# A two-layer trunk with a mixture of experts: the experts' gate and up products as plain fp32 in TensorE's four column groups, and x stored by ScalarE

## The chip, the cores and the metric

The kernel runs on one core of one Trainium2 chip, as one launch. The metric is the time of the launch on the device in microseconds (us); the median of three runs is what a change is judged by. A profile is one execution of its own, with one row for each instruction and each DMA packet. TensorE has two rows in it: PE for the products and PEld for the loads of their stationary side.

## The reference, cut to what matters

Two layers work on 640 tokens of 1,024 features: 512 latent ones and 128 context ones. Each layer has attention and a second mixer, and then a mixture of 16 experts. This part is what the change touches:

```
aff = softmax(x @ w_router, over tokens)
gate, idx = top_k(aff, cap)                # 64 latent + 16 context rows for an expert
xs  = x[idx]                               # 80 x 1024
hid = silu(xs @ w_gate) * (xs @ w_up)      # 1024 x 512 each
y   = (hid @ w_down) * gate                # 512 x 1024
out = zeros.at[idx].add(y)
```

Everything is fp32. An expert has 6 MB of weights and each is used once for a layer, so both layers together load 192 MB of them.

## The kernel before

**An expert's work.** The weights come in six blocks of 128 x 2048 values (1 MB): `g0 g1` (gate), `u0 u1` (up), `d0 d1` (down). To multiply fp32 values in one pass for each pair of operands, the kernel splits every value into a rounded part (`hi`, type fp32r) and a rest (`lo`), and computes `hi*hi + hi*lo + lo*hi` (`passes`, L1051). ScalarE writes `w_hi` from the loaded block (`expert_split`, L1953), VectorE subtracts it and writes `w_lo` (L2076). Three places of each of `w_hi` and `w_lo` go round (`SPLITS`). The 80 gathered rows are turned by TensorE (`turn_rows`, L1527) and split in the same way (`rows_split`), as is the turned hidden row (`hidden_split`). In `rows_times` (L1543) the 80 turned rows are the stationary side and 512 columns of a block the moving side: 8 slices of the 1,024 features, 3 passes, so 24 products of 512 columns for gate, 24 for up. Down has 24 more (`down_half`).

**Order on TensorE.** For each expert e (`step`, L1588): `gate(e+1)`, `turn_hidden(e)`, `up(e+1)`, `turn_rows(e+2)`, `down(e)`. Gate writes PSUM bank 4 or 5, up bank 3. ScalarE then makes `sig = silu(gate)` on 80 rows x 512, and VectorE `hid = up * sig`.

**Loads.** SyncE issues the blocks in the order in which TensorE uses them, into a ring of places: 8 in layer 0, 10 in layer 1 (`stage`, and stretches of `arena` and `xT`). A place may be filled again when VectorE has written the `w_lo` of the block in it (`lo_ready`, L783), which is before TensorE multiplies it. GpSimd gathers the rows of four experts ahead (`gather`) and adds the results in DRAM (`scatter`), each after the one before has landed.

**Start of the stage in layer 1.** x of five token tiles, evacuated to `x_out`, is stored into `acc_dram` by SyncE's queue just ahead of block 7 (L776 to L779), which waits for the stores to land because it is written over `x_out`. The final norm's gain (`gain_rows`, in the buffer `cs`) is loaded earlier, during layer 1's attention (L894).

## Time and profile before

| | |
|---|---|
| median of 3 runs | 1342.17 us (1340.73 to 1342.35) |
| profiled execution, its own time | 1343.86 us |
| span of its instructions | 1342.0 us |
| TensorE products | 7547, busy 1233.3 us (92%) |
| VectorE / ScalarE / GpSimd busy | 865.8 / 705.0 / 234.5 us |
| moved by DMA | 325 MB, mean 242 GB/s |
| experts' stage, layer 0: first product to last | 353.69 to 637.17 us |
| experts' stage, layer 1: first product to last | 1019.59 to 1310.10 us |

The products of TensorE overlap in their recorded durations, so the distance between two starts says what one costs, and a recorded duration does not. A DMA share near 1 means that all 16 DMA engines had packets in hand.

### The profile page before, as it was taken

How to read it: one execution, taken by the hardware profiler on the slowest of the kernel's cores; microseconds unless marked ns; L12 is line 12 of the kernel's file. 1: busy time of each engine (PE TensorE's matmuls, PEld its weight loads, DVE VectorE, ACT ScalarE, POOL GpSimd, SP SyncE). 2: the span in 40 equal slices, each digit the busy share in tenths (PEclk: the TensorE clock that was granted, in tenths of full speed). 3: DMA queues.
4: the chain of work that ended last, by engine and by line, in shares of the span. 5: the costliest groups of instructions: out<-in, count | busy, mean ns of one | idle time of the engine just before them, and what ended most of it. 6: DMA issues, size and time to landing. Idle time of an engine off the chain costs nothing.

```text
span 1342.0 us, 18162 instructions
## 1 busy us (share of the span) xinstructions
PE 1233.3 (92%) x7547; PEld 895.5 (67%) x7547; DVE 865.8 (65%) x1010; ACT 705.0 (53%) x821; POOL 234.5 (17%) x135
## 2 busy tenths in 40 slices
PE   5999988998599999999699998999986899999996
PEld 3898756796366666666389984668964566666662
DVE  4714566335588888887465252652355799998994
ACT  3522166413377777776343114653144677777762
POOL 3100000013212222211030000000232233333230
PEclk9899999999699999999899999999997999999996
DMA  9811371143999999999873230004258999999974
GB/s 362 268 63 65 102 262 32 64 157 135 338 401 375 383 385 383 386 391 380 279 237 110 63 121 23 2 1 158 95 185 297 421 385 384 385 386 383 391 283 166
DMA packets 100472, 324.98 MB, mean 242 GB/s; under 512 B 6720, under 2 KB 30495, under 8 KB 84007
## 3 DMA queue, kind: packets, MB, share of 16 engines
q1 hardware_dynamic: 90096, 293.51, 57.9%
q0 software_dynamic: 8400, 27.58, 8.0%
q10 hardware_dynamic: 1894, 2.73, 0.6%
q8 instruction: 60, 0.98, 0.3%
q14 instruction: 22, 0.17, 0.0%
HBM read 300.29 MB, written 23.50 MB: 241 GB/s over the span
## 4 chain that ended last, share of the span: by engine, by line
PE 66%; DMA 13%; DVE 10%; ACT 8%; issue 2%; POOL 1%; ACTq 0%; SPq 0%; DVEq 0%; POOLq 0%
PE psum L960 63%; DMA arena<-in_moe_w_up 4%; ACT arena L1885 4%; DMA acc_dram<-arena 4%; DVE w_lo L2076 2%; DVE arena L2372 2%; DMA stage<-in_moe_w_gate 2%; DMA arena<-in_moe_w_gate 2%; ACT w_hi L1957 1%; PE psum L1532 1%; ACT arena L1649 1%; POOL arena L830 1%; DMA h_hi<-h_dram,arena 1%; DVE arena L2113 1%; DVE arena L2493 1%
## 5 line engine op out<-in xcount | busy, mean ns | idle before, releaser
L960 PE MATMUL psum<-w_hi,h_hi 128*80 128x512 f32 (+1 forms) x848 | 330.1, 389 | 10.3 <-DVE w_lo L2076 6.6
L960 PE MATMUL psum<-w_lo,h_hi 128*80 128x512 f32 (+1 forms) x848 | 325.5, 384 | 0.0
L960 PE MATMUL psum<-w_hi,h_lo 128*80 128x512 f32 (+1 forms) x848 | 325.1, 383 | 0.0
L2076 DVE TENSOR_TENSOR w_lo<-stage,w_hi 128x2048 fp32r<-128x2048 f32 (+1 forms) x110 | 248.1, 2268 | 95.9 <-ACT w_hi L1662 59.3
L2076 DVE TENSOR_TENSOR w_lo<-arena,w_hi 128x2048 fp32r<-128x2048 f32 x87 | 198.5, 2288 | 34.8 <-ACT w_hi L1957 33.7
L960 PE MATMUL psum<-h_hi,w_hi 128*128 128x320 f32 x672 | 212.3, 316 | 1.5 <-DVE h_lo L2126 1.3
L960 PE MATMUL psum<-h_hi,w_lo 128*128 128x320 f32 x672 | 208.3, 310 | 0.0
L960 PE MATMUL psum<-h_lo,w_hi 128*128 128x320 f32 x672 | 208.2, 310 | 0.0
L1957 ACT ACTIVATE w_hi<-stage 128x2048 fp32r<-128x2048 f32 x88 | 167.2, 1914 | 43.7 <-PE psum L960 32.5
L923 POOL DMA_INDIRECT acc_dram<-arena x31 | 114.6, 3696 | 424.6 <-ACT arena L1998 220.0
L960 PEld LDWEIGHTS psum<-w_hi,h_hi 128*80 128x80 f32 (+1 forms) x848 | 129.8, 153 | 84.2 <-DVE w_lo L2076 13.9
L1957 ACT ACTIVATE w_hi<-arena 128x2048 fp32r<-128x2048 f32 x85 | 162.0, 1914 | 37.7 <-PE psum L960 18.0
L960 PEld LDWEIGHTS psum<-w_hi,h_lo 128*80 128x80 f32 (+1 forms) x848 | 129.7, 153 | 63.8 <-issue 1.4
L960 PEld LDWEIGHTS psum<-w_lo,h_hi 128*80 128x80 f32 (+1 forms) x848 | 130.1, 153 | 53.6 <-issue 1.2
L960 PE MATMUL psum<-arena 128*64 128x128 f32 (+6 forms) x964 | 137.9, 380 | 18.0 <-ACT arena L1885 10.4
L960 PEld LDWEIGHTS psum<-h_hi,w_hi 128*128 128x128 f32 x672 | 126.9, 189 | 8.4 <-issue 6.5
L960 PEld LDWEIGHTS psum<-arena 128*64 128x64 f32 (+3 forms) x964 | 78.4, 167 | 78.1 <-issue 50.3
L960 PEld LDWEIGHTS psum<-h_lo,w_hi 128*128 128x128 f32 x672 | 126.9, 189 | 0.5 <-issue 0.5
L960 PEld LDWEIGHTS psum<-h_hi,w_lo 128*128 128x128 f32 x672 | 126.7, 189 | 0.0
L1649 ACT ACTIVATE arena<-psum 128x512 f32<-128x512 f32 (+7 forms) x125 | 64.2, 575 | 88.5 <-PE psum L960 77.1
L1885 ACT ACTIVATE arena<-psum,arena 128x640 f32<-128x640 f32 x64 | 50.2, 789 | 57.9 <-DVE arena L2372 57.9
L1673 ACT ACTIVATE arena<-xT 128x640 f32<-128x640 f32 x24 | 17.7, 738 | 117.1 <-DVE xT L2430 87.4
(276 smaller groups left out, 1257.2 us busy)
## 6 DMA issues: line engine op xcount, KB each, us to landing
stage<-in_w_mod SPq DMA_DIRECT2D x46, 1024.0 KB, 7.2
stage<-in_moe_w_gate SPq DMA_DIRECT2D x32, 1024.0 KB, 17.9
arena<-in_moe_w_down SPq DMA_DIRECT2D x31, 1024.0 KB, 18.0
stage<-in_moe_w_up SPq DMA_DIRECT2D x30, 1024.0 KB, 17.2
arena<-in_moe_w_up SPq DMA_DIRECT2D x28, 1024.0 KB, 19.5
arena<-in_moe_w_gate SPq DMA_DIRECT2D x26, 1024.0 KB, 19.8
stage<-in_moe_w_down SPq DMA_DIRECT2D x26, 1024.0 KB, 19.1
xT<-in_moe_w_down SPq DMA_DIRECT2D x7, 1024.0 KB, 22.9
```

The costliest lines, as they stand in the source:

```text
L830: nc.gpsimd.tensor_tensor(rstd, rstd, sq[k % 2], ALU.add).then_inc(sq_added, 1)
L923: pool.indirect_dma_start(acc_dram[L], bass.IndirectOffsetOnAxis(slots[:, e:e + 1], 0), ysb[e % 2], None, compute_op=ALU.add).then_inc(sca ...
L960: return pe.matmul(o, w, x, start=first, stop=last, skip_group_check=True)
L1532: ins = pe.transpose(psum[:, k // 4, CAP * (k % 4):CAP * (k % 4) + CAP], xs[s][:, P * k:P * k + P], ident[0:CAP, 0:CAP])
L1649: freeing(nc.scalar.activation(dst, src, ACT.Copy, **kw))
L1673: nc.scalar.activation(rstd if k == 0 else sq[k % 2], xT[:, k, :], ACT.Square).then_inc(sq_ready, 1)
L1885: ins = nc.scalar.activation(p[:, LKEYS * a:LKEYS * a + LKEYS], src[:, 0:LKEYS], ACT.Exp, bias=largest(i, a), accum_out=total(i, a))
L1957: nc.scalar.activation(split_slot(w_hi, pc["q"]), slot(pc), ACT.Copy).then_inc(hi_ready, 1)
L2076: return nc.vector.tensor_tensor(dst, src, hi.bitcast(F32), ALU.subtract)
L2113: ins = nc.vector.scalar_tensor_tensor(hf[k % 2][:, grp], xT[:, k, grp], amul[:, L, 0, k, g:g + 1], rstd[:, grp], ALU.mult, ALU.mult)
L2372: ins = nc.vector.tensor_reduce(largest(i, a), src[:, 0:LKEYS], AX.X, ALU.max, negate=True)
L2493: then(nc.vector.max_index(idx[rows, c8], vals[rows, c8], from_))
```

## The change

The blocks of gate and up are no longer split. `rows_times` reads the loaded block itself and the turned rows as they are, with plain fp32 products. An fp32 product is two instructions of two passes each in the trace. The stationary side is 32 rows wide (or 16 for the last), so three products of 384 columns go into the column groups at rows 0, 32 and 64 of the array, and the remaining 128 columns of each of the three row groups go into the fourth group, at row 96, one after the other. So the gate result lies as 80 x 384, and in rows 96 to 127 as three pieces of 32 x 128. `silu` and the multiplication work on all 128 rows x 384. `turn_hidden` turns three blocks as before and gets the fourth by three small plain products from rows 96 to 127.

ScalarE and VectorE lose `expert_split` for g and u and VectorE loses `rows_split`; ScalarE copies the turned rows once (`rows_copy`). A place with a g or u block may be filled again only when TensorE has used it (`moe_used`). The turned rows of expert 1 go into `cs`, so `gain_rows` is loaded after the second scatter of layer 1. In layer 1 the x stores are issued by ScalarE's queue, and the order of lent places puts the front place ahead, so that the block that waits for the stores is block 8 (`d0` of expert 0). The wait of VectorE for the first gather (`first_gather_begun`) goes. The core of the diff:

```diff
-LENT_PLACES = {0: ..., 1: SUM_PLACES + X_PLACES + OUT_PLACES + (FRONT_PLACE,)}
+LENT_PLACES = {0: ..., 1: SUM_PLACES + X_PLACES + (FRONT_PLACE,) + OUT_PLACES}
+ROW_GROUPS, WIDE = (slice(0, 32), slice(32, 64), slice(64, CAP)), FF - P
...
-                            if n == OUT_PLACES[0] and L == LAYERS - 1:
-                                for t in range(NT):
-                                    emptied(sp, ("x out", t))
-                                    sp.dma_start(acc_dram[L][P * t:P * t + P, :], x_out[t]).then_inc(x_stored, 16)
                                 sp.wait_ge(x_stored, 16 * NT)
...
-                        sp.wait_ge(lo_ready, pc["earlier"]["q"] + 1)
+                        if pc["earlier"]["split"]:
+                            sp.wait_ge(lo_ready, pc["earlier"]["q"] + 1)
+                        else:
+                            used(sp, pc["earlier"])
...
                 def rows_times(e, what, b):
-                    hi, lo = expert_weights(e, what)
-                    half = int(what[1])
+                    pc, half = stream[moe_p[L] + piece_number(e, what)], int(what[1])
+                    pe.wait_ge(stage_in[pc["place"]], arrived(pc["p"]))
+                    w, x = slot(pc).rearrange("p (k n) -> p k n", k=4), rows_turned(e)
                     for k in range(4):
                         kk = 4 * half + k
-                        ins = passes(psum[0:CAP, b, :], tuple(t[:, kk, :] for t in x_pair(e)), (hi[:, k, :], lo[:, k, :]),
-                                     kk == 0, kk == KD - 1)
+                        for g, own in enumerate(ROW_GROUPS):
+                            mm(psum[96:96 + own.stop - own.start, b, P * g:P * g + P], x[:, kk, own], w[:, k, WIDE:FF],
+                               kk == 0 and g == 0, kk == KD - 1)
+                            ins = mm(psum[own, b, 0:WIDE], x[:, kk, own], w[:, k, 0:WIDE], kk == 0, kk == KD - 1)
...
                 def turn_hidden(e):
-                    for f in range(KF):
-                        ins = pe.transpose(psum[:, 2, CAP * f:CAP * f + CAP], hid[:, P * f:P * f + P], ident[0:CAP, 0:CAP])
+                    for f in range(KF - 1):
+                        pe.transpose(psum[:, 2, CAP * f:CAP * f + CAP], hid[0:CAP, P * f:P * f + P], ident[0:CAP, 0:CAP])
+                    for g, own in enumerate(ROW_GROUPS):
+                        last = slice(96, 96 + own.stop - own.start)
+                        at = CAP * (KF - 1) + own.start
+                        ins = mm(psum[:, 2, at:at + own.stop - own.start], hid[last, P * g:P * g + P], ident[last, last], True, True)
...
+                    for t in range(NT):
+                        emptied(act, ("x out", t))
+                        act.dma_start(acc_dram[L][P * t:P * t + P, :], x_out[t]).then_inc(x_stored, 16)
+
+                def rows_copy(e):
+                    act.wait_ge(rows_full, n0 + e + 1)
+                    nc.scalar.activation(rows_turned(e)..., psum[:, 0:2, 0:4 * CAP], ACT.Copy).then_inc(rows_copied, 1)
...
                 def step(e, more=True):             # ScalarE
-                    expert_split(plus(e, 1), "u0")
-                    ... rows_out(plus(e, -1))
-                    expert_split(plus(e, 1), "u1")
+                    if e:
+                        rows_out(e - 1)
+                    expert_split(e, "d0")
                     hidden_split(e)
-                    expert_split(e, "d0")
                     expert_split(e, "d1")
                     if more:
-                        rows_split(plus(e, 2))
-                    gate_silu(plus(e, 1))
-                    if more:
-                        expert_split(plus(e, 2), "g0")
-                        expert_split(plus(e, 2), "g1")
+                        rows_copy(e + 2)
+                    gate_silu(e + 1)
...
                 def step(e):                        # VectorE
                     if e:
                         rows_out(e - 1)
+                    expert_split(e, "d0")
                     hidden_split(e)
-                    expert_split(e, "d0")
                     expert_split(e, "d1")
-                    ... rows_split, expert_split(plus(e, 2), "g0"), hidden, expert_split(plus(e, 2), "g1")
+                    hidden(e + 1)
```

## Rows read from the trace of the kernel before

**Rows 1.** The chain that ended last, in layer 0: start, length, what.

```profile
449.28 11.23 PE psum L960 x48
...
466.86 11.22 PE psum L960 x48
```

**Rows 2.** Windows, layer 1: length, busy by engine (count), PE clock, DMA share, GB/s.

```profile
1100.00:1200.00 100.00, 100.00 (x479) 64.50 (x478) 92.70 (x58) 73.02 (x52) 38.48 (x12) 1.00 1.02 387
1031.00:1036.00 5.00, 5.00 (x23) 3.22 (x22) 4.72 (x4) 3.62 (x3) 0.00 (x0) 1.00 0.63 252
1036.00:1041.00 5.00, 5.00 (x26) 3.32 (x25) 1.71 (x1) 0.00 (x0) 0.00 (x0) 1.00 0.59 188
```

**Rows 3.** DMA issues of two windows (380 and 580 us on): size, time to landing.

```profile
arena<-in_moe_w_gate SPq DMA_DIRECT2D x2, 1024.0 KB, 12.8
...
stage<-in_moe_w_gate SPq DMA_DIRECT2D x2, 1024.0 KB, 19.1
```

**Rows 4.** Waits in the experts' stage of layer 1, TensorE, then SyncE's queue.

```profile
PE psum L960 <- DVE w_lo L2076: 6.1, 4, 4.9
...
SPq L789 <- DMA acc_dram<-arena: 25.4, 1, 25.4
```

**Rows 5.** Timeline of TensorE, expert 15 of layer 1: start, length, what.

```profile
1281.06 0.72 PE L1532 MATMUL psum<-cst,h_lo 80*128 80x80 f32 x8
1281.58 0.43 PE L960 MATMUL psum<-w_hi,h_hi 128*80 128x512 f32 x1
...
1287.28 0.43 PE L960 MATMUL psum<-w_hi,h_hi 128*80 128x512 f32 x1
...
1292.85 0.44 PE L1566 MATMUL psum<-cst,arena 80*128 80x80 f32 x4
1293.09 0.44 PE L960 MATMUL psum<-w_hi,h_hi 128*80 128x512 f32 x1
```

**Rows 6.** Timeline of TensorE, plain fp32: column groups, then a change of shape.

```profile
22.35 1.07 PE L960 MATMUL psum<-stage,sP 128*32 128x512 f32 x8 [1.44 <-DMA stage<-in_w_mod]
23.34 0.66 PE L1039 MATMUL psum<-cst,mrow 128*128 128x128 f32 x4
...
102.27 2.39 PE L960 MATMUL psum<-arena,small 128*32 128x512 f32 x20 [0.75 <-ACT arena L1649]
...
250.10 2.40 PE L960 MATMUL psum<-arena 128*64 128x128 f32 x40
```

**Rows 7.** Groups of instructions by shape, the same two products: count, busy us, mean ns.

```profile
L960 PE MATMUL psum<-stage,sP 128*32 128x512 f32 x368 | 46.5, 620 | 6.8 <-DMA stage<-in_w_mod 5.5 <-ACT arena L1998 1.2
...
L960 PE MATMUL psum<-arena 128*64 128x128 f32 x448 | 30.2, 277 | 1.7 <-DVE h_lo L2076 1.7
```

**Rows 8.** Timeline of the stationary loads, plain fp32, 128 columns, two row groups at a time.

```profile
831.02 0.30 PEld L960 LDWEIGHTS psum<-arena 64*128 64x128 f32 x4 [0.76 <-issue]
...
832.84 0.19 PEld L960 LDWEIGHTS psum<-arena 32*128 32x128 f32 x2 [0.24 <-issue]
```

**Rows 9.** Start of the stage in both layers, from the timeline.

```profile
352.81 0.82 DVE L2076 TENSOR_TENSOR h_lo<-psum,h_hi 128x640 fp32r<-128x640 f32 x1 [5.73 <-ACT h_hi L1980]
...
1009.12 2.56 SPq L778 DMA_DIRECT2D acc_dram<-arena  x5
...
1016.64 1.30 PE L1532 MATMUL psum<-cst,h_hi 80*128 80x80 f32 x8 [9.01 <-DMA h_hi<-h_dram,arena]
```

**Rows 10.** Costliest groups of the page: ScalarE's and VectorE's split of a block.

```profile
L2076 DVE TENSOR_TENSOR w_lo<-arena,w_hi 128x2048 fp32r<-128x2048 f32 x87 | 198.5, 2288 | 34.8 <-ACT w_hi L1957 33.7
...
L1957 ACT ACTIVATE w_hi<-stage 128x2048 fp32r<-128x2048 f32 x88 | 167.2, 1914 | 43.7 <-PE psum L960 32.5
```

**Rows 11.** The last block of each layer: time to landing, and layer 1's issue.

```profile
arena<-in_moe_w_down SPq DMA_DIRECT2D x1, 1024.0 KB, 18.0
...
1277.03 3.38 SPq L789 DMA_DIRECT2D xT<-in_moe_w_down  x1
...
xT<-in_moe_w_down SPq DMA_DIRECT2D x1, 1024.0 KB, 22.8
```

More of the change, by code:

```diff
@@ L383, in plan_weights @@
         for m in range(6 * E):
-            q = sum(x["split"] for x in stream)
-            stream.append(dict(key=(L, "moe", m), split=True, used=("moe_used", 6 * E * L + m + 1), p=len(stream), q=q, n=PIECE,
+            split = m >= 6 * E - 2 or (m >= 4 and (m - 4) % 6 >= 4)
+            q = sum(x["split"] for x in stream) if split else None
+            stream.append(dict(key=(L, "moe", m), split=split, used=("moe_used", 6 * E * L + m + 1), p=len(stream), q=q, n=PIECE,
                                place=rings[L][m % len(rings[L])]))
@@ L716, in trunk @@
         moe_p = [piece[(L, "moe", 0)]["p"] for L in range(LAYERS)]
-        moe_q = [piece[(L, "moe", 0)]["q"] for L in range(LAYERS)]
         def summed_rows(t):
@@ L924, in scatter @@
                                             compute_op=ALU.add).then_inc(scattered, 16)
-                gather(0)
-                pool.memset(stat[:, 15:16], 0.0).then_inc(first_gather_begun, 1)
-                for e in range(1, AHEAD):
+                for e in range(AHEAD):
                     gather(e)
@@ L940, in _ @@
                     scatter(e)
+                    if L == LAYERS - 1 and e == 1:
+                        pool.dma_start(gain_rows.rearrange("q (k p) -> q k p", k=KD),
+                                       a["final_norm"].rearrange("(o k p) -> o k p", o=1, p=P).to_broadcast([P, KD, P])).then_inc(gain_rows_in, 16)
                 if L == LAYERS - 1:
-                    pool.wait_ge(lo_ready, moe_q[L] + piece_number(E - 1, "d0") + 1)
+                    pool.wait_ge(moe_used, piece_number(E - 1, "u1", 6 * E * L + 1))
+                    pool.wait_ge(lo_ready, stream[moe_p[L] + piece_number(E - 1, "d0")]["q"] + 1)
                     pool.iota(one_hot, [[1, T]], base=0, channel_multiplier=0, allow_small_or_imprecise_dtypes=True).then_inc(token_numbers, 1)
@@ L1564, in turn_hidden @@
                     pe.wait_ge(hid_ready, lin(e, 1, n0 + 1))
-                    for f in range(KF):
-                        ins = pe.transpose(psum[:, 2, CAP * f:CAP * f + CAP], hid[:, P * f:P * f + P], ident[0:CAP, 0:CAP])
+                    for f in range(KF - 1):
[4 more added lines that the diff above has]
+                        ins = mm(psum[:, 2, at:at + own.stop - own.start], hid[last, P * g:P * g + P], ident[last, last], True, True)
                     ins.then_inc(hidT_full, 1)
                 def down_half(e, half):
-                    hi, lo = expert_weights(e, f"d{half}")
+                    pc = stream[moe_p[L] + piece_number(e, f"d{half}")]
+                    pe.wait_ge(lo_ready, pc["q"] + 1)
+                    hi, lo = (split_slot(t, pc["q"]).rearrange("p (k n) -> p k n", k=2) for t in (w_hi, w_lo))
                     for j in range(2):
@@ L1959, in _ @@
                 if L == 0:
-                    expert_split(0, "g0")
-                    expert_split(0, "g1")
                     act.wait_ge(new_out, 32)
@@ L1988, in gate_silu @@
                     act.wait_ge(moe_used, piece_number(e, "u1", 6 * n0 + 1))
-                    nc.scalar.activation(sig, psum[0:CAP, 4 + first(e) % 2, :], ACT.Silu).then_inc(silu_done, 1)
+                    nc.scalar.activation(sig, psum[:, 4 + first(e) % 2, 0:WIDE], ACT.Silu).then_inc(silu_done, 1)
                 def rows_out(e):
@@ L2001, in step @@
                 def step(e, more=True):
[L2002 to L2005 removed]
+                    if e:
+                        rows_out(e - 1)
+                    expert_split(e, "d0")
                     hidden_split(e)
[L2007 removed]
                     expert_split(e, "d1")
                     if more:
[L2010 to L2020 removed]
+                        rows_copy(e + 2)
+                    gate_silu(e + 1)
+                rows_copy(0)
+                rows_copy(1)
                 gate_silu(0)
@@ L2547, in rows_out, with step @@
                                                    gate_rows.rearrange("p (b n) -> p b n", b=2), ALU.mult, ALU.mult).then_inc(y_ready, 1)
[L2549 to L2551 removed]
+                def step(e):
                     if e:
                         rows_out(e - 1)
+                    expert_split(e, "d0")
                     hidden_split(e)
[L2555 removed]
                     expert_split(e, "d1")
[L2557 to L2572 removed]
+                    hidden(e + 1)
                 hidden(0)
@@ L2575, in _ @@
                     step(e)
-                step(E - 2, False)
+                step(E - 2)
                 expert_split(E - 1, "d0")
```

71 lines of the change are left out of this document (12 added, 59 removed).

## The prediction

> **What bounds the kernel now.** I read the chain of waits first. In both experts' stages it is TensorE's products almost throughout, and one expert follows the other at a fixed distance: 466.86 - 449.28 = 17.58 us [rows 1]. The windows say why: over 100 us of layer 1 TensorE is never idle [rows 2]. But it isn't alone. In the same window the DMA share is 1.02, and VectorE is at 93%. The third view, the DMA issues, shows how close the loads are. The same 1 MB block takes 12.8 us to land at 380 us and 19.1 at 580, while its issue keeps TensorE's pace [rows 3]. So the loads fall behind by about 6.3 us in 200 us, 0.5 us for an expert. Their own pace is near 18.1 us, and the lead from the stage's start covers the difference. The reader is to see two engines within 3% of each other, TensorE ahead only because it is fed from stock. Last, the waits: in layer 1 TensorE waits 6.1 us for `w_lo`, 4.9 of them at once, and SyncE stood 25.4 us on the landing of x ahead of the block that was missing [rows 4]. For 10 us around it the DMA share was only 0.6 [rows 2].
>
> **An expert on TensorE before** [rows 5]: turning the rows 0.52 us (1281.06 to 1281.58); down 5.70 and gate 5.57, both 24 products, so that 0.13 of down is a wait at its end; turning the hidden rows 0.24; up is the rest of 17.58, 5.55.
>
> **Gate and up after.** Per slice of features the fourth group gets three fp32 products of 128 columns, six instructions. The nearest row has 40 instructions of 128 columns in two halves of the array that run side by side, 20 in each, in 2.40 us [rows 6]; less 0.28 for the last one's duration [rows 7] that is 0.11 us each. Six are 0.66 us. The other groups get one product of 384 columns, two instructions. Eight instructions of 512 columns in four groups take 1.07 us in all [rows 6]: less the last one's 0.62 [rows 7] the second round starts 0.45 later, with a start-up in it; I take 0.44. Three quarters of 0.44, twice, is 0.66 as well. So the groups are balanced, if they run side by side, and a product of 8 slices takes 5.28 us.
>
> That they do is what everything hangs on, since the fourth group has three times as many instructions and they alternate with the others'. The head sums bear on this: ten products (20 instructions), each 512 followed by 128 columns in the same group and then the next group, took 2.39 us [rows 6]. One after the other they would need 10 x 0.44 + 10 x 0.11 = 5.5 us. So a later product of a free group passes an earlier one that waits for its own group. I take 0.66.
>
> The Trainium skill speaks against it: "TensorE: Matmul & The Clock Gate", section on the mechanism of packing, says matmuls are strict FIFO in start and end, and only weight loads are pulled ahead. By that page a product's second instruction would hold up all behind it. The head sums' row disagrees.
>
> **Changes of shape.** Two instructions of one shape overlap by 0.16 us in the record (0.39 long, 5.57 / 24 = 0.23 apart [rows 5]). Where the column groups give way to full width the overlap is 22.35 + 1.07 - 23.34 = 0.08, and the four turns behind it take 0.66 us, a step of 0.13 for 0.11 [rows 6]. So a change costs 0.08 and some 0.04 more: 0.12 us. After the change there are four of them for an expert (into gate, out to the hidden rows, into up, out to the rows), where there were none. Nothing hides them, since TensorE is the bound.
>
> **The hidden rows.** Three turns of four, 0.18 us, stay. The three small products are six instructions with a 128-column stationary side. Such a plain load follows the one before in its half after 0.30 - 0.19 = 0.11 us [rows 8] (four loads, two in each half, in 0.30; one alone in each, in 0.19), which is more than 32 columns need. So 6 x 0.11 = 0.66, and a change of shape of 0.1 ahead of them. With 0.12 for leaving the groups it is 1.06 us where it was 0.24. The trace has no such product behind another one; the bounds are 0.2 (loads hidden) and 1.0.
>
> **The sum for an expert:** gate 5.28 + 0.12, hidden rows 1.06, up 5.28 + 0.12, rows 0.52 + 0.12, down 5.70 - 0.13 = 18.07 us, which is 0.49 more than 17.58. Over 16 experts 7.8 us a layer.
>
> **What is taken from VectorE and ScalarE** is large and mostly off the path: four block splits, 4 x 2.29 us and 4 x 1.91 us [rows 10], an expert. The copies of the rows and of the hidden row stay on ScalarE behind `d0`, whose block TensorE needs no sooner than they. On the path there are two things. The first product no longer waits for VectorE's rest of the rows: -0.8 us in each layer [rows 9]. And the waits for `w_lo` in layer 1 go: -6.1 us [rows 4].
>
> **What comes in its place in layer 1.** The five stores, 2.5 MB, now go through ScalarE's queue. Before, they stood behind the loads in SyncE's, issued at 1009.12 [rows 9]. Beside the gathers they can delay the first one, for which TensorE waited 9.0 us: between 0 and 4 us (half as long again, as one queue of three where it was one of two); I take 1. The block behind their landing is now `d0` of expert 0. If they land as before (SyncE's wait ended at 1037) and the load takes 5 us and the two splits 4.2, it is ready at 1046.3. TensorE reaches it at 1018.8 + 1.7 (half clock at the start) + gate 5.4 + rows 0.64 + up 5.4 + gate 5.4 + 1.06 + up 5.4 + rows 0.64 = 1044.4. So up to 1.9 us remain of the wait, none if the stores land earlier; I take 1 (bounds 0 and 5). What queues behind that block on ScalarE is the copy of the hidden row and the rows of expert 2, none wanted sooner. ScalarE's five issues end before its first copy. The gain's load, half a block, costs 1.4 us of DMA time at 387 GB/s, hidden while TensorE is the bound.
>
> **Total:** layer 0: 7.8 - 0.8 = +7.0. Layer 1: 7.8 - 0.8 - 6.1 + 1 + 1 = +2.9. The tail behind the last scatter keeps its order. Together +9.9 on the profiled execution's own 1343.86, 1353.8. The median of the runs lies 1.7 below that execution, so 1352.1 us.
>
> **The rivals.**
>
> *The small terms come cheap and the loads become the bound (faster).* If the small products cost 0.2 instead of 0.66 and the changes of shape next to nothing, an expert takes 17.1 us. The balance tips at 17.58 + (0.8 + 0.8 + 6.1 - 2) / 32 = 17.76 us: below it the kernel gains. But then the loads hold it. The last block landed at about 609.9 + 18.0 = 627.9 and at 1277.03 + 22.8 = 1299.8 [rows 11]; its splits and 12 products of 0.23 end 7.0 us later, at 634.9 and 1306.8, against 637.2 and 1310.1. With the 4 us of idle DMA regained in layer 1, less 1.4 for the gain, that is -2.3 - 5.9 = -8.2: 1334. For it: the loads' lead is ample early on, and VectorE can't delay anything. Against it: all terms would have to be below their nearest rows. Chance 0.16. In between, a period of 17.7 to 17.8 leaves the time within 0.2%: 0.12.
>
> *The loads are late.* A gate or up place used to be free before its products; now it is held until TensorE has done with the block. At the start of layer 0, eight blocks are out and the ninth can't be issued before gate's first half is done. With a load pace of 18.1 us [rows 3] and less stock, TensorE would run behind each landing. At 18.5 us an expert it is 32 x 0.92 - 5.7 = +23.7 (5.7 being the gains less the costs at the starts): 1366. For it: the growing time to land. Against it: eight places are still 24 us of lead. Chance 0.12.
>
> *Instructions can't be issued fast enough.* A slice is 24 instructions (12 loads, 12 products) in 0.66 us, 27 ns each. The row of 40 products and 40 loads in 2.40 us is 30 ns [rows 6], but behind a short pause in which they could have queued, and here 192 follow without one. If a slice took 0.75 us, it would be 32 x 16 x 0.09 = +46 on top: 1398. Chance 0.05.
>
> The same page (section on the issue gap) gives 62 ns a matmul where decoding isn't in hardware, so 0.74 us for a slice by its figure, an estimate; no row here sustains a faster rate for long enough to exclude it.
>
> *The groups don't run side by side in this order.* Then a slice takes 3 x (0.11 + 0.33) = 1.32 us, and the total is 32 x 16 x 0.66 = 338 us more: about 1690. Against it the head sums. Chance 0.05.
>
> **How the numbers follow.** The forecast above has 0.5, with a range of its own of 1345 to 1360 (an expert between 17.85 and 18.3 us). Some 0.2% (2.7 us) is what a measurement of this kernel can tell from no change. Faster: 0.16. Same: 0.12. Slower: 0.5 + 0.12 + 0.05 + 0.05 = 0.72. The range reaches from 1337, which leaves out most of the faster rival, to 1376, beyond the late loads; the two last rivals stay outside.
>
> **What would show it.** The distance from expert to expert in the chain: 18.0, and 17.1 or 18.5 in the rivals. The distance between the starts of two slices in a gate product: 0.66, 0.75 or 1.32 us. The time between up's end and the hidden rows' last product, 1.06. The waits of TensorE in layer 1: one of about 1 us at `d0` of expert 0, and `w_lo` elsewhere none. Waits for DMA landings in TensorE's list would speak for the late loads. VectorE's busy share in the stage should fall to about 40%. The forecast is wrong if slices are not near 0.66 us, or if four changes and the small products cost under 0.6 us together.

## The result, and the profile after

The changed kernel takes 1369.28 us (median of 4 executions, 1360.51 to 1369.91), the kernel before 1342.26 beside it. The ratio is 1.0174, 95% interval 1.0144 to 1.0204: 23 us slower by the ratio, 27 by the medians. Five rounds on another chip gave 1368.36 against 1343.83, 1.0186 (1.0157 to 1.0216). The forecast was 1352.1, slower; direction and range hold, but the loss is more than twice the 9.9 us that the sum gave. The profiled execution took 1369.91 us, with a span of 1368.1.

The page after, its first part (columns: busy time, share, instructions), shows what was taken from VectorE and ScalarE. TensorE is busy longer (1233.3 us before), and it is the only engine that is:

```profile
span 1368.1 us, 27280 instructions
## 1 busy us (share of the span) xinstructions
PE 1263.6 (92%) x12315; PEld 1019.8 (75%) x12315; DVE 558.2 (41%) x850; ACT 462.7 (34%) x693; POOL 168.6 (12%) x133
```

The chain of waits in layer 0 answers to [rows 1]. Again TensorE alone, again a fixed distance, now 537.42 - 518.93 = 18.49 us:

```profile
518.93 0.36 PE psum L1559 x3
519.29 6.35 PE psum L958 x55
525.63 0.70 PE psum L1530 x8
526.34 11.08 PE psum L958 x73
537.42 0.36 PE psum L1559 x3
537.78 6.35 PE psum L958 x55
```

TensorE's timeline over the same expert answers to [rows 5] (start, duration of the group, products):

```profile
518.86 0.43 PE L1559 MATMUL psum<-cst,arena 80*128 80x80 f32 x3
519.22 0.84 PE L958 MATMUL psum<-cst,arena 32*128 32x32 f32 x6
519.98 5.65 PE L958 MATMUL psum<-arena 128*32 128x128 f32 x96
525.57 0.77 PE L1530 MATMUL psum<-cst,h_lo 80*128 80x80 f32 x8
526.13 0.43 PE L958 MATMUL psum<-w_hi,h_hi 128*80 128x512 f32 x1
...
531.77 5.65 PE L958 MATMUL psum<-stage,arena 128*32 128x128 f32 x96
537.35 0.43 PE L1559 MATMUL psum<-cst,arena 80*128 80x80 f32 x3
```

Read the starts: up 519.98 to 525.57 = 5.59, rows 0.56, down 5.64, gate 5.58, hidden rows 0.36 + 0.76. The 96 instructions are 8 slices of 12. Six starts of the fourth group, 0.109 apart, make a slice of 0.655 us, and eight slices 5.24. So the groups do run side by side, as forecast, and 0.34 us more passes before anything of full width can start.

The windows answer to [rows 2]. TensorE is nearly as full as before (98.25 of 100 us) and at full clock, the DMA share is as high, and VectorE has fallen from 93% to 36%:

```profile
1100.00:1200.00 100.00, 98.25 (x1195) 79.02 (x1196) 35.90 (x27) 27.03 (x27) 11.79 (x10) 1.00 1.02 378
```

TensorE's waits in layer 1 answer to [rows 4]: of 6.1 us for `w_lo`, 1.7 are left. The 1.3 us for `h_lo` are the wait at `d0` of expert 0, seen from its last link. TensorE waited 1.3 us longer for the first gather than before.

```profile
PE psum L1530 <- DMA h_hi<-h_dram,arena: 10.3, 1, 10.3
...
PE psum L958 <- DVE w_lo L2064: 1.7, 2, 1.0
...
PE psum L958 <- DVE h_lo L2064: 1.3, 1, 1.3
```

**The stages of every profile**, in us. A stage runs from the start of its first turn of rows to the end of its last down product; "between" is what lies between the two stages. "An expert" is the distance by the chain where nothing is waited for.

| profile | an expert | layer 0 | between | layer 1 | median us |
|---|---|---|---|---|---|
| before | 17.58 | 286.4 | 379.5 | 293.5 | 1342.2 |
| before, again (e7) | 17.58 | 285.0 | 380.9 | 290.8 | 1343.98 |
| changed | 18.49 | 299.8 | 385.0 | 302.5 | 1369.28 |
| changed, again (e0) | 18.49 | 298.7 | 383.7 | 301.9 | 1368.36 |
| e1 large first | 18.12 | 293.3 | 383.3 | 300.8 | 1358.45 |
| e2 two thirds behind | 18.06 | 292.4 | 380.7 | 302.6 | 1358.70 |
| e3 hidden rows ahead | 18.05 | 293.0 | 380.1 | 300.8 | 1358.39 |
| e4 small turns | 18.01 | 293.3 | 379.4 | 300.2 | 1357.40 |
| e5 all three | 17.33 | 290.5 | 378.5 | 299.6 | 1353.57 |
| e6 stores by SyncE | 18.49 | 299.5 | 383.5 | 305.0 | 1369.12 |
| e8 all three, half loads | 17.32 | 281.9 | 378.2 | 285.5 | 1327.3 (one) |
| e9 changed, half loads | 18.49 | 299.7 | 383.2 | 303.0 | 1366.9 (one) |
| e10 before, half loads | 17.58 | 285.1 | 380.9 | 291.0 | 1340.1 (one) |
| e11 before, front first | 17.58 | 284.9 | 381.6 | 295.1 | 1344.59 |
| e12 before, padded | 18.49 | 300.4 | 380.5 | 305.4 | 1366.58 |
| e13 padded in layer 0 | 18.49, 17.58 | 300.7 | 381.0 | 294.4 | 1360.84 |

### The profile page after: what moved, and what is told of

The parts are those of the page before. It is cut to its first block, busy times and chain, and to the rows that moved or that the text cites. A ratio compares the mean times of both kernels' runs of the same rounds, so it can differ in the third digit from the quotient of the medians.

```text
span 1368.1 us, 27280 instructions
## 1 busy us (share of the span) xinstructions
PE 1263.6 (92%) x12315; PEld 1019.8 (75%) x12315; DVE 558.2 (41%) x850; ACT 462.7 (34%) x693; POOL 168.6 (12%) x133
## 4 chain that ended last, share of the span: by engine, by line
PE 73%; DMA 9%; DVE 7%; ACT 7%; issue 2%; POOL 1%; ACTq 1%; DVEq 0%; POOLq 0%; SPq 0%
PE psum L958 69%; DMA arena<-in_moe_w_down 4%; ACT arena L1884 4%; DMA acc_dram<-arena 4%; DVE arena L2360 2%; PE psum L1530 1%; DVE w_lo L2064 1%; ACT arena L1648 1%; POOL arena L829 1%; PE psum L1559 1%; DMA h_hi<-h_dram,arena 1%; PE psum L1360 1%; DVE arena L2481 1%; DVE arena L2480 0%; DVE arena L2483 0%
## 5 line engine op out<-in xcount | busy, mean ns | idle before, releaser
L958 PE MATMUL psum<-arena 128*32 128x384 f32 (+8 forms) x3268 | 277.8, 382 | 18.5 <-ACT arena L1884 10.1
L958 PEld LDWEIGHTS psum<-arena 128*32 128x32 f32 (+5 forms) x3268 | 200.2, 123 | 87.5 <-issue 56.0
L958 PE MATMUL psum<-stage,arena 128*32 128x384 f32 (+3 forms) x3060 | 190.0, 387 | 2.4 <-ACT arena L1976 1.6
L958 PEld LDWEIGHTS psum<-stage,arena 128*32 128x32 f32 (+1 forms) x3060 | 165.4, 107 | 16.8 <-issue 7.7
L2064 DVE TENSOR_TENSOR w_lo<-stage,w_hi 128x2048 fp32r<-128x2048 f32 (+1 forms) x48 | 107.5, 2246 | 147.2 <-ACT w_hi L1956 87.4
L958 PE MATMUL psum<-w_hi,h_hi 128*80 128x512 f32 (+1 forms) x336 | 124.7, 371 | 3.1 <-DVE w_lo L2064 1.7
L2064 DVE TENSOR_TENSOR w_lo<-arena,w_hi 128x2048 fp32r<-128x2048 f32 x33 | 75.6, 2292 | 117.3 <-ACT w_hi L1956 116.9
L958 PE MATMUL psum<-w_hi,h_lo 128*80 128x512 f32 (+1 forms) x336 | 122.8, 366 | 0.0
L958 PE MATMUL psum<-w_lo,h_hi 128*80 128x512 f32 (+1 forms) x336 | 122.7, 365 | 0.0
L1956 ACT ACTIVATE w_hi<-stage 128x2048 fp32r<-128x2048 f32 x26 | 49.5, 1906 | 59.0 <-DMA stage<-in_moe_w_down 59.0
```

Source lines behind the costliest of these rows:

```text
L958: return pe.matmul(o, w, x, start=first, stop=last, skip_group_check=True)
L1956: nc.scalar.activation(split_slot(w_hi, pc["q"]), slot(pc), ACT.Copy).then_inc(hi_ready, 1)
L2064: return nc.vector.tensor_tensor(dst, src, hi.bitcast(F32), ALU.subtract)
```

## The experiments

**e0: the changed kernel again.**

> The changed kernel once more, unaltered. Its executions so far were 1369.91, 1368.9, 1369.65 and 1360.51 us, at granted clocks of 0.967, 0.967, 0.967 and 0.971. Theory: between the two experts' stages part of the extra time is TensorE's clock and not the change: in the profiled execution the products of 840.7 to 860 us ran at half clock (granted clock 0.52 at 841 to 844, 0.50 at 853 to 856) where the same products of the kernel before ran at 1.00, which cost 4.4 us. Then executions fall into two levels some 4 to 9 us apart, and the higher goes with the lower granted clock. Rival: the 1360.51 was a chance and all executions lie within 0.2% of 1369.

Measured: 1363.61 to 1372.4 us in six executions, median 1368.36, clocks 0.962 to 0.972. There are no two levels: the times are spread evenly over 9 us, and the kernel before on the same chip is spread over as much (1337.17 to 1345.95 in 11). The highest time has the lowest clock (0.962) and the lowest the highest (0.972), but 1364.59 stands at 0.968 and 1367.45 at 0.970. Clock plays a part in the scatter; my two levels fall.

**e1 and e2: the order within a slice.**

```
-  for g, own in enumerate(ROW_GROUPS):
-      mm(psum[96:..., b, P*g:P*g+P], x[:, kk, own], w[:, k, WIDE:FF], ...)
-      ins = mm(psum[own, b, 0:WIDE], x[:, kk, own], w[:, k, 0:WIDE], ...)
+  for g, own in enumerate(ROW_GROUPS):          # e1; in e2 the small one of g == 0 stands ahead of these
+      mm(psum[own, b, 0:WIDE], ...)
+  for g, own in enumerate(ROW_GROUPS):
+      ins = mm(psum[96:..., b, P*g:P*g+P], ...)
```

> In each slice the three products of 384 columns come first and the fourth group's three products of 128 columns behind them. Theory (stagger): in the changed kernel a slice takes 0.655 us as forecast, but the third group's product starts 0.23 to 0.30 us after the others', because it stands behind the fourth group's second product in the queue; that lag is paid when a product of 8 slices ends, 5.58 us instead of 5.33. With the large ones first all groups start together: 0.25 us less for each of the 64 products, 16 us, so about 1353. Rival (the end is inherent): leaving the column groups for the whole array costs 0.34 us whatever the order: 1369, product 5.58. Second rival (small ones held back): the fourth group's first product now stands behind three waiting second instructions; if it can't pass them, a slice takes 0.33 + 0.66 = 0.98 us, a product 7.9 and the kernel about 1520.

> In each slice: the fourth group's first small product, then the three of 384 columns, then its other two. Theory (stagger): the third group's product now stands behind one small product instead of three and starts within 0.02 us of the others; 5.33 us a product, 1353. Rival (the end is inherent): 1369. Against the kernel with all three large ones first it tells whether the small ones can pass waiting instructions: if not, this one is at 1353 to 1370 and that one at 1520.

Measured: e1 1358.45 us, ratio to before 1.0123 (1.0098 to 1.0149); e2 1358.7, 1.0114 (1.0073 to 1.0155); the changed kernel beside them 1.0186. The product shrank from 5.58 to 5.38 in e1 and to 5.36 in e2 (515.51 - 510.15 below). TensorE's timeline of e2:

```profile
510.15 5.43 PE L958 MATMUL psum<-arena 128*32 128x128 f32 x96
515.51 0.42 PE L1564 MATMUL psum<-cst,arena 80*128 80x80 f32 x3
515.86 0.84 PE L958 MATMUL psum<-cst,arena 32*128 32x32 f32 x6
516.63 5.43 PE L958 MATMUL psum<-arena 128*32 128x128 f32 x96
521.99 0.77 PE L1530 MATMUL psum<-cst,h_lo 80*128 80x80 f32 x8
```

That the lag is the third group's can be seen in the groups of instructions by shape, in a window of 0.14 us at the start of up. In the changed kernel (520.06 to 520.20) the third group's product, the one with 16 stationary columns (128\*16), isn't running:

```profile
L958 PE MATMUL psum<-arena 128*32 128x384 f32 x2 | 0.5, 510 | 0.0
L958 PE MATMUL psum<-arena 128*32 128x128 f32 x2 | 0.4, 284 | 0.0
```

It comes in the window from 520.22 on, 0.23 us behind the others. In e2 it starts 0.02 us behind the product's first instruction, and is there in the window of 516.62 to 516.76:

```profile
L958 PE MATMUL psum<-arena 128*32 128x384 f32 x2 | 0.5, 510 | 0.0
L958 PE MATMUL psum<-arena 128*16 128x384 f32 x1 | 0.5, 497 | 0.0
L958 PE MATMUL psum<-arena 128*32 128x128 f32 x1 | 0.3, 297 | 0.0
```

So the stagger is real and its price is 0.20 to 0.22 us for a product, where I expected 0.25. The rivals fall. The end isn't inherent, and the small products pass three waiting instructions. But of 16 us expected only 10 came (1368.4 - 1358.5). Layer 0 gave the 6 that 16 x 0.37 makes; layer 1, with the same TensorE time saved, gave 1.4 in e1 and nothing in e2. In e2 most of it went at one place, `d0` of expert 0, the block behind the landing of x: TensorE waited 5.5 us there, where it waited 1.3 in the changed kernel, and then ran at a granted clock of 0.50, where the changed kernel had 1.00. The waits for `w_lo` were 2.6 us for 1.7.

**e3: the hidden rows turned ahead of gate.**

```
   def step(e, more=True):
+      if e:
+          turn_hidden(e)
       gate(plus(e, 1))
-      turn_hidden(e)
+      if not e:
+          turn_hidden(e)
       up(plus(e, 1))
```

> The hidden rows of an expert are turned directly behind the down product of the one before, ahead of the next gate product instead of between gate and up (except for the first expert of a layer). Then gate and up follow one another in the same shape, and one leaving of the groups and one entry fall away for an expert. Theory: that saves the 0.34 us that leaving costs and about 0.1 for entering, less 0.1 for a further change within the rows: 0.35 x 30 = 10 us, 1359. Rival: the hidden row isn't ready (VectorE's product of it comes behind the split of d1), TensorE waits 0.3 us or more there, and nothing is gained: 1369.

Measured: 1358.39 us, 1.0124 (1.0096 to 1.0151), as expected, though by some luck: the two stages gave 6.2 and 1.4 us, and the rest of the 10 came between them (380.1 us). Gate and up together take 10.82 us instead of 2 x 5.58, the three turns 0.30 instead of 0.36. The hidden row is ready: no wait appears at it.

**e4: the small products as turns.**

```
-  ins = mm(psum[:, 2, at:...], hid[last, P*g:P*g+P], ident[last, last], True, True)
+  ins = pe.transpose(psum[:, 2, at:...], hid[last, P*g:P*g+P], ident[last, last])
```

> The hidden rows' three small products (six instructions in fp32) become three turns of one instruction each. In the changed kernel the six start 0.112 us apart and the way from the third turn to the up product is 0.357 + 0.767 us. Theory (loads of 128 columns set the step): three instructions less, 3 x 0.11 = 0.33 us an expert, 10.7 us in all if nothing else holds: 1358. Rival (each wait for the row group, not the count, sets it): no gain, 1369. From the runs before: once an expert takes near 18.1 us the down blocks come late in layer 1, so that layer may give back up to 4 us: 1358 to 1362.

Measured: 1357.4 us, 1.0109 (1.0082 to 1.0137). From the first small one to the next product it is 0.29 us instead of 0.77, 0.48 less and not 0.33: the three turns start closer together than the six fp32 instructions did. In layer 1 the waits for `w_lo` are now 4.1 us and the one at `d0` of expert 0 is 2.1, and that layer gives 2 us where TensorE saved 7.7.

**e5: the three edits together** (in the order of e2).

> The three edits at once: one small product, the three large ones, the two other small ones; the hidden rows turned behind the down product before; and the small products as turns. TensorE alone would then need 18.49 - 0.45 (between gate and up) - 2 x 0.22 (less 0.22, as only one product of the two is left with a leaving) - 0.33 = about 17.4 us an expert, under the kernel before with 17.58. Theory (loads are the next bound): layer 0 has its stock and takes 16 x 17.4, layer 1 has not: it took 298.7 us in both of the faster variants though TensorE's own period had fallen to 18.05 (288.8 for 16), and stays there. Then 1369 - 16 x 1.1 (layer 0) - 3 = about 1348 to 1350, slower than before. Rival (TensorE alone): 1369 - 32 x 1.1 = 1334.

Measured: 1353.57 us, 1.008 (1.0057 to 1.0103): still slower than before, though TensorE now needs only 17.33 us for an expert. That is 3.6 us above the range that I expected. Layer 0 has no stock for the whole stage either: it gave 8.8 us where 17.6 were expected. The chain of waits of e5 in layer 1 tells why (start, duration, what). It goes through the down blocks, each on its way for some 24 us, and then their splits:

```profile
1077.34 5.37 PE psum L958 x48
...
1082.73 23.37 DMA arena<-in_moe_w_down
...
1106.12 1.92 ACT w_hi L1964
...
1108.07 2.30 DVE w_lo L2072
...
1110.42 3.02 PE psum L958 x12
...
1113.93 5.37 PE psum L958 x48
...
1119.32 24.52 DMA arena<-in_moe_w_down
...
1143.87 1.92 ACT w_hi L1964
```

**e8, e9, e10: half the loads.** From the eleventh block of a layer on, these kernels leave out the second half of every load.

```
   into = slot(pc).rearrange("p (k n) -> p k n", k=src.shape[1])
+  if m >= SLOTS + len(lent_places):
+      into, src = into[:, 0:src.shape[1] // 2], src[:, 0:src.shape[1] // 2]
   sp.dma_start(into, src).then_inc(stage_in[n], 16)
```

> The kernel with all three edits, but from the eleventh block of a layer on each load brings only the first half of its block (0.5 MB), so that the experts' stages compute with old data in the other half. Everything else, order and waits, is kept. Theory (loads are the bound of that kernel): TensorE then runs at its own pace, 10.60 + 0.30 + 0.29 + 0.57 + 5.57 = 17.33 us an expert; with some 2 us of start a stage takes 280 us from the first turn of rows on plus 2.5, where it was 290.5 and 299.6; the whole about 1353.6 - 8 - 17 = 1329. Rival (something on TensorE or its feeding engines other than loads): 1345 to 1354.

> The changed kernel with the same halved loads. Theory: in layer 0 it is bound by TensorE alone and stays at 298.7 to 299.8 us for the stage; in layer 1 only the 1.3 to 3.1 us of waits for down blocks go, 302 to 299. The whole 1364 to 1368. Rival (loads cost it too): 10 us or more less, 1358.

> The kernel before with the same halved loads. Theory: its TensorE needs 17.58 us an expert and its layer 0 stays at 285 to 286 us; layer 1 loses only the wait behind the stores of x, at most 6 us: 1337 to 1343. Rival (the kernel before is held by the loads already): layer 0 falls by more than 2 us. Beside the kernel with all three edits it says what the change would be worth if loads cost nothing: 1329 against 1338.

Measured (one execution each): e8 1327.3, e9 1366.9, e10 1340.1 us. The windows of 400 to 600 us and 1100 to 1200 us first in e5, then in e8 (columns as in [rows 2]: the last three are granted clock, DMA share and GB/s):

```profile
400.00:600.00 200.00, 195.13 (x2535) 164.47 (x2534) 60.15 (x44) 69.15 (x66) 24.87 (x21) 0.98 1.02 380
1100.00:1200.00 100.00, 95.49 (x1260) 80.89 (x1252) 36.96 (x28) 30.66 (x30) 11.72 (x10) 0.98 1.02 376
```

```profile
400.00:600.00 200.00, 200.00 (x2690) 171.94 (x2692) 64.85 (x47) 72.36 (x70) 46.21 (x22) 1.00 0.73 217
1100.00:1200.00 100.00, 100.00 (x1361) 86.28 (x1354) 39.25 (x30) 30.08 (x30) 39.99 (x12) 1.00 0.71 215
```

With full loads TensorE stands still for 2.4% and 4.5% of these stretches and the DMA share is 1.02; with half of them it never stops. The stages fall by 8.6 and 14.1 us. So the loads are what holds e5. With half of them it is 12.8 us faster than the kernel before with half of them (e10), in one execution of each; the two stages make 8.7 of that, and most of the rest lies between them. The changed kernel as it was given doesn't move in layer 0 (299.7 for 299.8 and 298.7), nor in layer 1 (303.0 for 302.5 and 301.9), so the loads have no part in its loss in layer 0. The kernel before doesn't move in layer 0 either. The waits of 1.7 us for `w_lo` that I meant to see leave layer 1 in e9 did leave, but no time came out of it. It was given back at `d0` of expert 0: the wait was 1.7 us for 1.3, and the products behind it ran at half clock, where in the changed kernel the same window of 1064 to 1066 us has a clock of 1.00:

```profile
1064.00:1066.00 2.00, 2.00 (x6) 1.25 (x5) 1.69 (x2) 0.00 (x0) 0.00 (x0) 0.50 1.02 412
```

From the turn of rows before them to the next it took 22.0 us in e9 and 20.1 in the changed kernel, 1.9 more.

**e6: x stored by SyncE again**, in front of `d0` of expert 0, with the loop of five stores moved from ScalarE's block back to SyncE's.

> x is stored by SyncE again, in front of d0 of expert 0 of layer 1, all else as changed. Theory (as forecast): ScalarE's stores cost at most 1 us at the first gather of layer 1 (10.3 us of waiting in the changed kernel, 9.0 before) and land when they did before (SyncE's wait for them ended 16.3 us later in a kernel that was 16.3 later), so the time is within 2 us of 1369. Rival (the stores on ScalarE matter): they begin earlier by ScalarE and free d0's place sooner; on SyncE the wait at d0 of expert 0 (1.3 us) grows by 5 or more, 1374.

Measured: 1369.12 us, 1.0197 (1.0167 to 1.0226), the same as the changed kernel. The wait at `d0` of expert 0 is 3.7 us for 1.3, and the stage 2.5 to 3 longer in this profile, which the median doesn't show. So the stores' engine is no cause of the loss.

**e7: the kernel before again.**

> The kernel before once more, for a second profile. Between the last product of layer 0's experts and the first turn of rows of layer 1's it took 379.5 us in its first profile, the changed kernel and its three variants 385.0, 383.7, 383.3, 380.7 and 380.1, over the same instructions. Theory (clock by chance): this stretch varies with the granted clock in each execution, and the kernel before shows it too: a value between 379 and 385 with half-clock stretches at other places. Rival (the change shifts something in it): 379.5 again.

Measured: 1341.93 us, and 380.9 between the stages (the median in the table is that of the runs of the kernel before on that chip). The stretch is 1.4 us longer than in the first profile, and the clock has its part in it. The 28 products behind the pause at 827 us, at full clock in the first profile, ran in part at half here. Windows of 828 to 836 us, first profile and second:

```profile
828.00:836.00 8.00, 5.57 (x28) 2.90 (x28) 3.05 (x5) 5.04 (x13) 0.00 (x0) 1.00 0.16 56
```

```profile
828.00:836.00 8.00, 7.21 (x28) 3.30 (x28) 2.70 (x5) 3.51 (x8) 0.00 (x0) 0.79 0.10 33
```

**e11: the kernel before with the front's place first.** One line of the change alone, the order of places in `LENT_PLACES[1]`.

> The kernel before with one line of the change alone: in layer 1 the front's place comes ahead of the two that wait for the landing of x, so the block behind that wait is d0 of expert 0 and no longer u1 of expert 1. Theory: the wait of 4.9 us for u1 of expert 1 goes, as d0 is ready at 1046.3 and needed at 1047; the loads' own pace then takes part of it back, since the last block can't land much before 1299.8: 2 to 3.5 us faster, 1340 to 1342 against 1343.9. Rival (the loads take all of it back): no difference.

Measured: 1344.59 us, 1.0008 (0.9991 to 1.0026): no difference. In its profile the wait of 4.9 us at `u1` of expert 1 is gone, and eight waits for `w_lo` sum to 6.7 us. But more than half of them is the old wait at its new place. SyncE's wait for the landing of x ended at 1040.1 us (before 1037.1), `w_lo` of `d0` was ready at 1049.3 and not at 1046.3, and TensorE stood there:

```profile
1049.45 0.69 PE L960 MATMUL psum<-w_hi,h_hi 128*80 128x512 f32 x1 [3.59 <-DVE w_lo L2076]
```

So the rival had the number. Of its mechanism, loads that take the gain back later, the profile shows 3.1 us at other blocks, where the kernel before had 1.2.

**e12, e13: the kernel before, padded to the changed one's distance.**

```
-  for k in range(KD):                       # turn_rows
+  for k in 2 * tuple(range(KD)):            # e13: in layer 0 alone
-  for f in range(KF):                       # turn_hidden
+  for f in (0, *range(KF), *range(KF)):     # e13: in layer 0 alone
```

> The kernel before with 13 turns more for an expert (the eight turns of its rows made twice, the hidden rows' four twice and one of them a third time; the same results), 0.07 us each, so that TensorE needs 17.58 + 0.91 = 18.49 us as after the change, with everything else as before. Theory (the distance from expert to expert is all that counts): layer 0's stage takes 16 x 0.91 = 14.6 us more, 285.7 to 300; layer 1's the same less the 6.1 us of waits at most, 292 to 302; the whole 1366 to 1369. Rival for the stretch between the stages: if the 3 to 5 us there come from the change itself, this kernel has 379.5 to 381 as the kernel before and ends at 1363 to 1366; if they go with the longer stage, it has 383 to 385.

> The same in layer 0 alone. Theory: layer 0's stage 300, layer 1's 291 to 293.5 as before: 1343.9 + 14.6 = 1358, or 1361 to 1363 if the stretch between the stages is 383 to 385 once layer 0 ends later.

Measured: e12 1366.58 us, 1.0178 (1.0143 to 1.0213); e13 1360.84, 1.0124 (1.009 to 1.0158). The chain of waits of e12 shows the distance, 509.96 - 491.47 = 18.49 us:

```profile
491.47 1.11 PE psum L1532 x16
492.58 11.23 PE psum L960 x48
503.81 0.62 PE psum L1566 x9
504.44 5.52 PE psum L960 x24
509.96 1.11 PE psum L1532 x16
```

Thirteen idle turns for an expert, and nothing else, make the kernel before as slow as the changed one, within the intervals. It isn't as slow in the same places. In its profile layer 0 takes 1.1 us more than in the changed kernel's two and layer 1 3.2 more, with one wait of 4.0 us at `u1` of expert 1 behind the stores; layer 1's 305.4 also lies above the 292 to 302 that I expected. Between the stages both padded kernels have 380.5 and 381.0, which is 3 to 4 less than the changed one, so the longer stage isn't what makes 383 to 385 there. e13 is 3 us slower than the 1358 of its expectation; of its stages layer 0 is as expected and layer 1 1 us above, and the rest stays open.

## Why the prediction was right in direction and wrong in size

**What bounds the kernel**: right, and more so than I used it. TensorE sets the pace (e9, e10: halving the loads moves no stage of layer 0). And the next bound stands right behind it: e1 to e4 saved 0.37 to 0.48 us an expert on TensorE, and layer 1 stayed at 300 to 303 us with waits for landed blocks.

**A slice of 0.66 us, balanced, side by side**: right, 0.655. The two rivals that hung on it, instructions that can't be issued fast enough and groups that don't run side by side, are out. A later product of a free group does pass earlier ones that wait, as I read out of the head sums, in e1 past three of them. The Trainium skill ("TensorE: Matmul & The Clock Gate", the mechanism of packing) has matmuls strictly in order. The trace disagrees. Instruction by instruction, in the up product at 519.98 us the first and the second large product start at 519.99 and 520.00, and the small product's second instruction, which stands ahead of both in the queue, at 520.12. The Trainium skill's 62 ns a matmul (the same page, the back-to-back issue gap), which made 0.74 us of a slice by an estimate, did not bind here: 96 instructions with as many loads ran at 0.655 us a slice, 55 ns each, without a pause. The page gives that figure for decoding outside the hardware; which way these were decoded no run shows.

**The step that failed: "a product of 8 slices takes 5.28 us", with 0.12 for leaving the groups.** It is a term of the sum that was mis-sized; its mechanism, balanced groups, was right. I priced only the change of shape there, and took the groups as starting and ending together. Measured from the first product to the first turn behind it, it is 5.58, against 5.28 + 0.12 = 5.40. Within it the eight slices were right (5.24), and leaving the groups, priced at 0.12, took 0.34. In the order of the code the third group's large product stands last, behind all three small products and the two other large ones, and starts 0.23 us late; within the product the lag stays, since all groups step alike. The last instructions of the three large groups start at 524.95, 524.85 and, in the third, 525.15, and full width follows behind that last one. With one small product ahead of it (e2) it starts with the others, and the product takes 5.36, which is my 5.40 within 0.04. Two such products an expert: 2 x 0.18 = 0.36 of the 0.42 us by which an expert was under-priced. The trace of before had no row with three equal groups beside a fuller one; my bounds for the small terms came from rows where all groups had the same load, so they couldn't hold this.

**The other terms of an expert.** Down with the entry into gate 5.64 (forecast 5.57 + 0.12, 0.05 too high); hidden rows with the entry into up 1.12 (forecast 1.06, with leaving gate's groups counted in it; cut as here 0.94 + 0.12); rows 0.57 (0.52). Six fp32 instructions of the small products do start 0.11 us apart, as the plain loads of [rows 8] said. The sum of the differences is 0.18 + 0.18 - 0.05 + 0.06 + 0.05 = 0.42 us, and over 32 experts 13.4 us of the 15 to 17 that were missing (27.0 or 24.5 by the medians, less 9.9). The rest is 1.4 us in layer 1 and about 3 between the stages, both below. By the profiles this is 1 to 3 us more than the medians want, which is within their scatter.

**The first product without VectorE's rest of the rows**: right. From the first turn of rows to the first product of layer 0 it was 353.69 - 350.73 = 2.96 us, now 355.32 - 353.23 = 2.09 (e0), 0.87 less where 0.8 was forecast. Layer 0's stage follows from the two: 16 x 0.91 - 0.87 = 13.7, measured 299.3 - 285.7 = 13.6.

**Layer 1**: forecast 7.8 - 0.8 - 6.1 + 1 = 1.9 us more for the stage, measured 302.2 - 292.2 = 10.0 (means of the two profiles each). The distance accounts for 6.7 of the 8.1. For the other 1.4: I took 6.1 us of waits as removed and 1 as put in their place. The second profile of before has only 3.6 us of waits for `w_lo` and a stage 2.7 us shorter, so I priced the gain from one execution with more of them than the next; and 1.7 us of `w_lo` waits remained where I had forecast none. The wait at `d0` of expert 0 was right, 1.3 us and 0.4 in e0, forecast 1. Its bounds of 0 and 5 were needed, since the variants have up to 5.5 (e2). What I hadn't priced is the clock behind such a wait: after the 4.9 us at `u1` of expert 1 the kernel before has a granted clock of 0.50 from 1048 to 1050 us, and the changed kernel, with 1.3 us of waiting, 1.00 from 1056 to 1072.

**The gathers**: TensorE waited for the first one 10.3 us in the changed kernel and 9.0 before, 1.3 more where 1 was taken. In other profiles it was 8.2 (e12) and 8.7 (e7) in the old kind, 8.6 (e9) in the new with half the loads. So about 1 us, with scatter as large.

**Between the stages** I forecast nothing beyond the gathers. The kernel before has 379.5 and 380.9, the changed one 385.0 and 383.7. What the 3 to 4 us are can be shown, and why they come stays open. The whole stretch in before and in the changed kernel (the clock is the third from the end):

```profile
637.17:1016.64 379.47, 342.36 (x2488) 274.81 (x2489) 181.06 (x345) 146.56 (x253) 41.31 (x39) 0.98 0.37 123
648.97:1033.92 384.95, 348.07 (x2488) 280.04 (x2489) 176.78 (x343) 141.43 (x250) 39.04 (x39) 0.95 0.36 120
```

In the changed kernel's first profile 4.4 us more than before lie in one place. From the first product behind the pause that e7 shows at 827 us to the start of a group three steps on it took 862.88 - 840.74 = 22.14 us by the chain of waits, before 846.88 - 829.11 = 17.77. There the products ran at a granted clock of 0.79 and 0.62 (windows of 840 to 848 and 852 to 860 us) after a pause of the same length as before (2.05 and 2.04 us):

```profile
840.00:848.00 8.00, 7.21 (x28) 3.35 (x28) 2.52 (x5) 3.51 (x9) 0.00 (x0) 0.79 0.00 0
852.00:860.00 8.00, 8.00 (x48) 5.53 (x44) 3.43 (x6) 3.51 (x8) 0.00 (x0) 0.62 0.00 0
```

That it goes with the clock, all 16 profiles show. The five whose stretch takes 383.2 us or more (changed, e0, e1, e6, e9) have a granted clock of 0.50 or 0.51 in the window of 203 to 208 us behind the end of layer 0's stage. e11 and e13 (381.6 and 381.0) have 0.71 and 0.63 there, and the other nine (378.2 to 380.9) 1.00. Why the clock falls there isn't shown. The changed gate and up aren't enough for it, since e3 and e4 have them and lie at 380.1 and 379.4, and neither is the longer stage (e12, e13). The medians don't bound it: the padded kernel is as slow as the changed one (1.0178 and 1.0186), but with stages that take 4.3 us more in its profile.

**The rivals.** The late loads (1366) came nearest in microseconds, for the wrong reason: in the changed kernel no landing delays TensorE in layer 0, and half the loads change nothing there. That rival's mechanism is real one step further on, in e5. The cheap small terms with the loads as the bound (1334) is what e5 made come true: TensorE needs 17.33 us, and the kernel is still 1.008 of before. I had put that case 8.2 us ahead of before, taking the landings as they were. They are no fixed quantity.

**Why e5 doesn't win.** Layer 0's last block lands at 632.1 us in e5 and at 627.8 in before, with the DMA share at 1.02 in both from 350 us on; between 1100 and 1200 us the same share moves 376 GB/s, before 387 [rows 2]. That stretch shows the largest difference. From 360 to 627 us it is 382 against 385, and from 1060 to 1280 us 381 against 388. The places of gate and up are held until TensorE has read them, where a split freed them earlier. Whether the lower rate comes from that or from which engines read beside the transfers wasn't tried. Beside the rate there is the one block behind the landing of x: in layer 1 TensorE waits 3.7 us for it in e5, and from 1052 to 1056 us, behind that wait, the granted clock is 0.50.

## What to carry to other kernels

- When column groups carry unequal numbers of instructions, put the one large product of each group first in the queue and the many small ones behind: the groups then start together, and the lag of the last one isn't paid each time the array goes back to full width (0.2 us here, 64 times).
- Price a product from its first start to the first start of what follows it, not as slices times a slice. Then halve the loads in an experiment and see what moves. That run says whether the loads hold this kernel (e8 against e5: yes, 8.6 and 14.1 us), but not how near they are when nothing moves: e10 moved nothing in layer 0, and yet e5, with 0.25 us less of TensorE an expert than the kernel before, was held by them.
- A padded kernel before (idle work that brings only the new pace) separates what an iteration costs from everything else a change touches. Compare it stage by stage, since equal medians can hide differences that cancel (4.3 us more in the stages and 3 to 4 less between them here).
- A block that is late costs more than its wait. Behind the waits at the start of layer 1 the kernel before, e2, e5 and e9 ran at half clock for some products, and the changed kernel, with 1.3 us of waiting, did not. A wait can also be moved from one block to another without getting shorter (e11).

## What the runs showed of the hardware that was not expected

- Instructions for a free column group pass others that wait for theirs, but not without limit. In the changed kernel the third group's first instruction stands behind seven that hadn't started at 520.00 us. It started at 520.23, 0.006 us behind the fourth group's third instruction, with five still waiting ahead of it. Behind three waiting ones an instruction started at once (e1, product 5.38 us for 5.58, and e2). What exactly the limit counts wasn't tried.
- A plain fp32 product with a stationary side of 128 columns costs two starts 0.11 us apart even for 32 rows. From the first of three such products to the product behind them it was 0.77 us, from the first of three turns of the same size 0.29 (e4).
- At a DMA share of 1.02 the rate wasn't constant: 387 GB/s in the kernel before, 378 in the changed one and 376 in e5 from 1100 to 1200 us. From 360 to 627 us it was 385, 378 and 382.
